# The place of the expert sums in TensorE's order: 1.05 slots behind the dot in place of 1.6

## What is computed

```python
def peer(h, w_pq, keys, u_tab, v_tab):
    ...
        q = (hb @ w_pq).reshape(t, P_HEADS, 2, P_QDIM // 2)
        sc = jnp.einsum('thpd,hpkd->thpk', q, keys).astype(jnp.float32)
        sv, si = lax.top_k(sc, P_TOPK)
        cand = (sv[:, :, 0, :, None] + sv[:, :, 1, None, :]).reshape(t, P_HEADS, P_TOPK * P_TOPK)
        ...
        cv, ci = lax.top_k(cand, P_TOPK)
        eidx = jnp.take_along_axis(cidx, ci, axis=-1)
        gate = jax.nn.softmax(cv, axis=-1)
        act = jax.nn.gelu(jnp.einsum('thkd,td->thk', u_tab[eidx], hb).astype(jnp.float32))
        return jnp.einsum('thk,thkd->td', (gate * act).astype(hb.dtype), v_tab[eidx])
```

## Time and profile before

| | |
|---|---|
| median of 3 runs | 5308.55 us (5306.74 to 5311.1) |
| the profiled execution | 5301.91 us |
| its span, first to last instruction | 5299.8 us |
| TensorE (PE) busy with matmuls | 4119.2 us, 78% |
| VectorE (DVE) busy | 2892.1 us, 55% |
| ScalarE (ACT) busy | 1633.3 us, 31% |
| GpSimd (POOL) busy | 1563.7 us, 30% |
| software queue (the gathers) | 1342.26 MB, 62.1% of the 16 DMA engines' time |
| hardware queue (weights and the rest) | 294.07 MB, 14.2% |
| mean granted TensorE clock | 0.849 |

### The profile page before, as it was taken

How to read it: one execution, slowest core, us unless ns; L and a number is a source line. 1 busy time by engine, 2 the same in 40 slices (tenths; PEclk the granted TensorE clock), 3 DMA queues, 4 the chain that set the end, 5 groups by cost and what they waited for, 6 DMA issues and landing times.

```text
span 5299.8 us, 62841 instructions
## 1 busy us (share of the span) xinstructions
PE 4119.2 (78%) x20590; PEld 1765.3 (33%) x20590; DVE 2892.1 (55%) x6283; ACT 1633.3 (31%) x4857; POOL 1563.7 (30%) x1454
## 2 busy tenths in 40 slices
PE   4988999977887766666669889998778877666666
PEld 2554883332223311111125547733322233111111
DVE  2441443477566776654445324334866677766544
ACT  0210442223333333333322104422233333333333
POOL 0220002233333444433322100022333344444432
PEclk5998999988998967666679899999889999777666
DMA  6115109988999999999951250198999999999998
GB/s 259 49 60 214 49 1 354 350 339 344 421 421 399 420 420 421 421 421 421 421 239 47 81 217 14 49 380 333 354 351 421 421 392 420 421 421 421 421 421 353
DMA packets 232594, 1640.35 MB, mean 310 GB/s; under 512 B 26704, under 2 KB 29008, under 8 KB 36944
## 3 DMA queue, kind: packets, MB, share of 16 engines
q0 software_dynamic: 184320, 1342.26, 62.1%
q1 hardware_dynamic: 47952, 294.07, 14.2%
HBM read 1632.95 MB, written 3.28 MB: 309 GB/s over the span
## 4 chain that ended last, share of the span: by engine, by line
PE 39%; DMA 37%; DVE 15%; issue 4%; ACT 3%; DVEq 2%; POOL 1%; SPq 0%; ACTq 0%; POOLq 0%
DMA arena<-in_experts,arena 24%; PE ps L717 13%; DMA front<-in_experts,arena 8%; PE ps L941 8%; DVE sq L1390 6%; DMA arena<-in_weights 5%; PE ps L848 3%; PE ps L871 3%; PE ps L917 3%; PE ps L893 2%; PE ps L906 2%; PE ps L861 2%; DVE arena L1138 1%; ACT arena L1075 1%; DVE arena L1141 1%
## 5 line engine op out<-in xcount | busy, mean ns | idle before, releaser
L941 PE MATMUL ps<-arena 64*64 64x512 f32 x9040 | 1578.3, 779 | 806.5 <-ACT arena L1075 793.4
L695 POOL DMA_INDIRECT arena<-in_experts,arena x1130 | 1263.4, 1118 | 2885.6 <-PE ps L941 1910.7
L1390 DVE CUSTOM_DVE_ANT_0 sq<-arena 128x1024 f32<-128x1024 f32 x1130 | 1385.8, 1226 | 886.3 <-DMA arena<-in_experts,arena 807.3
L941 PEld LDWEIGHTS ps<-arena 64*64 64x64 f32 x9040 | 311.7, 156 | 1909.4 <-issue 1886.8
L1069 ACT ACTIVATE arena<-arena 128x1 f32<-128x1 f32 x1280 | 258.3, 202 | 2069.5 <-DVE arena L1390 2068.2
L717 PE MATMUL ps<-arena 128*128 128x512 f32 (+3 forms) x1920 | 828.9, 579 | 75.5 <-DMA arena<-in_weights 73.6
L1075 ACT ACTIVATE arena<-ident,arena 128x128 f32<-128x128 f32 x1280 | 514.0, 402 | 91.4 <-issue 3.5
L717 PEld LDWEIGHTS ps<-arena 128*128 128x128 f32 x1920 | 360.7, 196 | 526.8 <-issue 476.7
L1071 ACT ACTIVATE arena<-arena 128x1 f32<-128x1 f32 x1280 | 376.7, 294 | 90.7 <-issue 3.5
L917 PE MATMUL ps<-arena 128*128 128x256 f32 (+1 forms) x1536 | 352.3, 374 | 6.3 <-issue 2.3
L917 PEld LDWEIGHTS ps<-arena 128*128 128x128 f32 x1536 | 254.3, 201 | 185.7 <-issue 152.2
(11 more groups left out here) (150 smaller groups left out, 3126.3 us busy)
## 6 DMA issues: line engine op xcount, KB each, us to landing
arena<-in_weights SPq DMA_DIRECT2D x242, 1024.0 KB, 8.9
arena<-in_experts,arena POOLq DMA_INDIRECT x1130, 20.5
arena<-mod_rows SPq DMA_DIRECT2D x24, 512.0 KB, 6.7
arena<-in_weights SPq DMA_DIRECT2D x8, 576.0 KB, 6.1
arena<-in_keysT SPq DMA_DIRECT2D x4, 1024.0 KB, 12.9
arena<-in_weights SPq DMA_DIRECT2D x4, 768.0 KB, 9.0
arena<-in_g_norm SPq DMA_DIRECT2D x6, 512.0 KB, 9.7
arena<-in_weights SPq DMA_DIRECT2D x6, 512.0 KB, 4.7
```

The lines of the kernel that those rows point to most:

```text
L695: pool.indirect_dma_start(out=ring[BUF[n]], out_offset=None, in_=ins["experts"], in_offset=bass.IndirectOffsetOnAxis(ap=index(t)[:, slot:s ...
L941: last = MM(acc[h][to:to + 64, c * 512:(c + 1) * 512], diag[n % 4][lo:lo + 64, lo:lo + 64], ring[BUF[n]][lo:lo + 64, D + c * 512:D + (c + ...
L1390: V.tensor_tensor_reduce(out=sq[:], in0=ring[BUF[n]][:, 0:D], in1=h2_of_slot(n), scale=1.0, scalar=0.0, op0=ALU.mult, op1=ALU.add, accum_o ...
```

## The change

The points of all sums, and of what is placed relative to them (`ex`, `ea`, `sw`, `ew`), move 0.55 slots forward.

```diff
@@ -245,7 +245,7 @@
         return [i for _, i in sorted(self.points, key=lambda p: p[0])]
 
 
-LAG = 1.6
+LAG = 1.05
 
 
 def schedule():
```

## The result

| | before | after |
|---|---|---|
| median of 4 runs | 5307.65 us | 5434.53 us (5431.61 to 5438.32) |
| span of the profiled execution | 5299.8 us | 5429.5 us |
| mean granted TensorE clock | 0.849 | 0.842 |

The ratio is 1.024, with a 95% interval of 1.0223 to 1.0258: 127 us slower, where 60 were forecast and 94 were the range's upper end. The direction was right, the size was not.

What follows compares the result with a forecast made beforehand. DMA's gathers were taken to bound the full stretches, leaving some 970 us of 5300 to decide. Merge, routing and tile-end terms, 2 x (5 + 24 + 1) = 60 us on 5308.6, gave 5368; range 5322 to 5402.

Steps and rivals of the forecast that it cites:

- the pair without room behind its score: Routing stretch: 15 of 16 pairs of top-16 searches a layer begin just when the score is evicted, so VectorE has no room.
- 24 us a layer: Routing stretch: eight pairs of searches cost 12 us, sixteen 24, because scores come later behind the moved sums.
- The replay's chain: Routing stretch, worked from dot 78: dot, diagonal, sums, score, eviction in series; pair 4 begins 2.0 late, pair 5 4.6.
- In the full stretches ... is covered: Tile ends in stretches with DMA full (share 1.01 and 1.00): the queued gathers cover the extra diagonal of 1.08 us.
- the full stretches keep their length: Sign to look for: stretches with DMA full, 1300 to 2700 us and 3950 to the end, only start later.
- The bounds of the sum: Routing cost a layer: 9 us (nine passed scores at 1.0 us) to 38 us (fourteen at 2.7).
- The merge stretch, 5 us a layer: Slots 0 to 56: sums passing pieces of projections make TensorE wait for diagonals; 5 us a layer, between 0 and 12.
- The tile ends, 1 us a layer: A diagonal now follows `ex` before the new tile's first sums; uncovered only at a layer's first boundary, 1 us a layer.
- No cost for the buffers and banks: From slot 117 some gathers exchange buffers 3 and 6, and two PSUM banks change places; neither changes a size: no cost.
- Nothing gives it back.: Routing delay stays: later dots mean later sums and gathers while DMA is below full; afterwards it is full and can't catch up.
- The rival of sooner releases: Merge stretch: buffers return sooner and DMA fills up, winning at most TensorE's idle time, 13.4 and 12.9 us: 5282; chance 0.11.
- The rival of the clock: Routing stretch: longer waits leave TensorE at its low clock, 20 more blocks of sums a layer, 36 us: 5404; chance 0.15.

Runs made afterwards that it cites:

- the run that keeps them and loses nothing: The kernel after (sums at 1.05, its buffers and banks) with dot and diagonal also moved 0.55 slots forward: 5298.44 us, ratio 0.9992.

## Why the prediction was half right

- *Which way, and by what.* Right: the moved sums, the pair without room behind its score, VectorE's waits as the place where it shows. The forecast of the waits (19 to 40 or more) came out at 51.
- *"24 us a layer" in the first routing stretch.* 30, by the slot table and by the run of those slots alone. The replay's chain is in the trace; it lacked the low clock (1.3 us in the first of its pairs). The first score of the stretch was evicted 7.2 us later (1082.9 to 1090.1 us), but 6.0 of these were there at slot 57 already, so the stretch's start added 1.2. To the eighth score 14.1 us more were lost, and from there to the sixteenth 15.3. So either half of the pairs cost 15.3 us, where the replay had 12 for one and I took 12 for the other.
- *"In the full stretches ... is covered", and "the full stretches keep their length".* This step failed, and it is most of the miss of 67 us: 41 us for both layers. I read DMA's share of 1.01 as unlimited cover. It was cover for 28.5 us of waits in the second routing stretch of layer 0; the chain there asked for 44. The bounds of the sum held no term for it, so the range didn't either.
- *The merge stretch, 5 us a layer.* 5.8 and 3.7 by slot, which fits, but two executions of the same order differ there by as much, so its size is confirmed only roughly. But the tiles' second merge, from slot 118, has the same pattern, and its start lost 10 us a layer (14 us for both layers in the run of those slots alone). It lay at the edge of what I counted as full. I had cut the change at the DMA row and not at the items passed.
- *The tile ends, 1 us a layer.* Nothing that shows, and too small for these runs to tell.
- *No cost for the buffers and banks.* Right, by the run that keeps them and loses nothing.
- *"Nothing gives it back."* Not quite: 6.1 and 5.0 us came back between slots 320 and 352. DMA's share there is 1.01 before and after, but VectorE's waits for landings fell from 9.5 to 2.2 us (6.9 to 0.9 in layer 1): this fits gathers that had got ahead while the dots were late.
- *The rival of sooner releases.* Not seen anywhere; freeing buffers later (2.2) cost nothing either. The prediction took DMA as the most contended over the span; by busy time that was close, 76.3% for its two large queues beside 78% for TensorE. The rule of the Trainium skill (Perfetto Trace Analysis, Identifying the Most-Contended Engine) was read as pointing at DMA. Its next section, on tracing a gap to what the engine waits for, is the one that fits. In the routing stretch DMA's share fell from 0.87 to 0.79 as a consequence of VectorE's waits.
- *The rival of the clock.* A part of the chain, and not what starts it: the granted clock of the stretch went from 0.87 to 0.85, in layer 1 from 0.87 to 0.82. How many microseconds of the 127 are its doing was not separated.

By slots and runs the sum would have been 2 x (5 + 30 + 9) + 41 = 129 us, against 127 measured; the 41 is what the second routing stretches cost net of what came back behind them. Of the miss of 67 us that gives 41 to the second routing, some 14 to the start of the second merge and some 12 to the first routing.

## What to carry to other kernels

Where each engine runs its part of one list in order, look for the consumer that starts the moment its input is there, and don't put a wait ahead of what feeds it: here an engine that was idle a quarter of the time (TensorE) set the pace through a score of 0.6 us. A stretch in which DMA is full covered at most the microseconds that VectorE waited for landings there (33.5 us, of which 28.5 were given up); read that number before costing a delay at nothing. It is an upper bound: behind slot 118 there were 11.7 us of such waits, and a delay of 9.2 us was hardly covered. And give such a consumer one step of room: taking the search one query later won 19 us of the kernel before, and cut what moving the sums to 1.05 costs from 127 us to 33.

## What had not been expected

The sums' distance to their dot has a knee: 1.05, 1.3, 1.6 and 2.2 slots give 5434.5, 5366.9, 5307 and 5304.0 us. From 1.6 to 2.2 slots it buys nothing; below 1.6 it costs over 200 us per slot (62 us for 0.3, 127 for 0.55). These are four points of one schedule, and where between 1.3 and 2.2 the knee lies was not measured.
